# Hybrid attention decoder step on one core: sample sums one step earlier, projection's first block split anew, state copies inside the projection's loop

## The reference, cut to what matters

```python
def mixer_prompt(h, w_in, cw, g_sb, g_nsa, w_out):
    q_sb, k_sb, v_sb, q_n, kv_c, kv_s, kv_w, gates = project(h, w_in, pos)   # z = h @ w_in
    o_sb = sb_prompt(q_sb, k_sb, v_sb)                                        # stick-breaking attention
    ...                                                                       # compressed, selected and window attention
    out = mixer_out(o_sb, o_n, g_sb, g_nsa, w_out)

def sb_attend(q, k, v, q_pos, k_pos):
    z = jnp.einsum('bqhd,bshd->bhqs', q, k) / math.sqrt(HEAD_DIM)
    mask = k_pos[None, :] < q_pos[:, None]
    log_1m = jnp.where(mask, jax.nn.log_sigmoid(-z), 0.0)
    after = lax.cumsum(log_1m, axis=3, reverse=True) - log_1m
    a = jnp.where(mask, jnp.exp(jax.nn.log_sigmoid(z) + after), 0.0)
    return jnp.einsum('bhqs,bshd->bqhd', a, v)

# samples: the same over the gathered pages of the caches, and
win_all = jnp.concatenate([win_buf, kv_w], axis=1)
new_win_kv_sample = win_all[:, W + T - n_keep:]        # the window state, shifted by one row
```

## Time and profile before

| | us |
|---|---|
| median of 3 runs | 1145.65 |
| lowest, highest | 1145.42, 1149.24 |
| the profiled execution | 1144.81 |
| its span in the trace | 1143.0 |
| PE busy in the span | 1061.2 (93%) |
| DVE, ACT, POOL busy | 619.5, 391.3, 63.3 |
| mean granted clock of TensorE | 0.943 of full |

### The profile page before, as it was taken

The page is one execution under the profiler, slowest core; times in us unless marked ns, Lnnn a source line. Parts: engine busy times, 40 slices in busy tenths (PEclk is TensorE's granted clock), DMA queues, the critical chain, the costliest instruction groups (busy, mean ns, idle before and its releaser), DMA issues.

```text
span 1143.0 us, 22964 instructions
## 1 busy us (share of the span) xinstructions
PE 1061.2 (93%) x8284; PEld 933.5 (82%) x8284; DVE 619.5 (54%) x1056; ACT 391.3 (34%) x729; POOL 63.3 (6%) x83
## 2 busy tenths in 40 slices
PE   6899998988989998899999889999999999998995
PEld 5899997887878886555555558999999999998995
DVE  5334664777768776775455445445533335553334
ACT  4111122333333335656454354322221112222124
POOL 1000003111111100000000000100000000000000
PEclk8899996989989895999998999999999999999998
DMA  8427539999999853356666762223333332333221
GB/s 295 151 89 201 129 98 227 250 248 258 269 261 260 246 182 120 121 175 226 204 208 194 214 203 75 75 74 92 110 92 91 92 83 84 91 92 93 90 78 75
DMA packets 180323, 177.59 MB, mean 155 GB/s; under 512 B 13128, under 2 KB 140869, under 8 KB 177893
## 3 DMA queue, kind: packets, MB, share of 16 engines
q1 hardware_dynamic: 178536, 169.72, 52.5%
q10 hardware_dynamic: 1724, 7.04, 1.8%
HBM read 170.83 MB, written 10.06 MB: 158 GB/s over the span
## 4 chain that ended last, share of the span: by engine, by line
PE 61%; SPq 18%; issue 7%; DVE 5%; DMA 5%; ACT 3%; ACTq 1%; POOL 0%; DVEq 0%; POOLq 0%
PE bank L664 59%; SPq L578 4%; SPq L499 3%; SPq L542 3%; SPq L545 3%; PE bank L668 3%; SPq L492 2%; DMA high_arena<-in_w_in_dram 2%; SPq L566 2%; DMA low_arena<-in_cache_nsa_slc_kv_dram 1%; DMA low_arena<-in_consts_dram 1%; DMA high_arena<-out_cmp_p_dram 1%; ACTq L1284 1%; DVE high_arena L2231 0%; DMA high_arena<-in_cache_nsa_slc_kv_dram 0%
## 5 line engine op out<-in xcount | busy, mean ns | idle before, releaser
L664 PE MATMUL bank<-high_arena 128*128 128x254 f32 (+8 forms) x1864 | 242.0, 349 | 11.9 <-ACT high_arena L1321 6.1
L664 PEld LDWEIGHTS bank<-high_arena 128*128 128x128 f32 (+5 forms) x1864 | 186.9, 153 | 49.8 <-issue 9.2
L2163 DVE TENSOR_TENSOR w_low<-high_arena,w_high 128x1024 fp32r<-128x1024 f32 x72 | 90.1, 1252 | 81.0 <-ACT w_high L1484 71.0
L1484 ACT ACTIVATE w_high<-high_arena 128x1024 fp32r<-128x1024 f32 x72 | 76.4, 1061 | 144.7 <-PE bank L664 144.7
L668 PE MATMUL bank<-low_arena 128*128 128x128 f32 (+3 forms) x658 | 103.2, 298 | 16.4 <-DMA low_arena<-in_cache_nsa_slc_kv_dram 10.4
L664 PE MATMUL bank<-a_high,w_high 128*128 128x256 f32 (+1 forms) x512 | 103.7, 284 | 5.3 <-issue 2.9
L668 PEld LDWEIGHTS bank<-low_arena 128*128 128x128 f32 (+3 forms) x658 | 83.0, 157 | 28.9 <-issue 12.3
L664 PE MATMUL bank<-h_high,w_high 128*128 128x256 f32 (+1 forms) x512 | 103.0, 282 | 1.8 <-DVE h_low L2187 1.8
L664 PE MATMUL bank<-a_low,w_high 128*128 128x256 f32 (+1 forms) x512 | 103.2, 283 | 0.0
L664 PE MATMUL bank<-h_low,w_high 128*128 128x256 f32 (+1 forms) x512 | 103.2, 283 | 0.0
L664 PE MATMUL bank<-h_high,w_low 128*128 128x256 f32 (+1 forms) x512 | 103.1, 283 | 0.0
(11 more groups left out here) (227 smaller groups left out, 1541.2 us busy)
## 6 DMA issues: line engine op xcount, KB each, us to landing
low_arena<-in_cache_sb_kv_dram SPq DMA_DIRECT2D x128, 256.0 KB, 4.8
high_arena<-in_cache_sb_kv_dram SPq DMA_DIRECT2D x128, 256.0 KB, 3.5
high_arena<-in_cache_nsa_cmp_kv_dram SPq DMA_DIRECT2D x128, 128.0 KB, 5.0
high_arena<-in_w_up_dram SPq DMA_DIRECT2D x32, 512.0 KB, 4.0
high_arena<-in_w_down_dram SPq DMA_DIRECT2D x32, 512.0 KB, 4.0
high_arena<-in_w_in_dram SPq DMA_DIRECT2D x10, 1136.0 KB, 5.9
low_arena<-in_cache_nsa_slc_kv_dram SPq DMA_DIRECT2D x128, 64.0 KB
high_arena<-in_cache_nsa_slc_kv_dram SPq DMA_DIRECT2D x128, 64.0 KB, 2.3
```

The source lines that it names most:

```text
L664: return T.matmul(out, lhsT=l, rhs=r, start=start, stop=stop, **k)
L1484: S.activation(w_hi_r[u], w_raw[u], ACT.Copy).then_inc(sem(f"w_hi{u}"), 1)
L2163: V.tensor_tensor(w_lo_r[u], w_raw[u], w_hi[u], ALU.subtract).then_inc(sem(f"w_lo{u}"), 1)
```

## The change

Three independent parts.

1. **First block of the projection.** The low parts are cut into four pieces of two k each: DVE k 0 and 1, ahead of its `gained_low` loop (and no longer within it), POOL k 2 and 3, then k 4 and 5, then k 6 and 7. PE waits for `w_lo0` at k = 0 and for `z_zero` 2, 3, 4 at k = 2, 4, 6.
2. **State copies.** The eight copies leave their place ahead of the loop; one is issued by ACT behind the eviction of rows 3 of each of blocks 0 to 7.
3. **Steps.** `sample_sums`, `sample_logs` go from step 3 to step 2, the Exp and the memset of bank 7 from step 4 to step 3, the first pairs from step 5 to step 4. Samples 0 to 3 keep 3, 3, 2 pairs in three steps each, one step earlier; sample 4 has 3, 1, 1, 1, 0, 1, 0, 1 in steps 16 to 23 where it had 2 and six times 1 in steps 17 to 23. From step 24 on the table is as before.

```diff
-    at = 5
+    at = 4
...
-        for n in ((3, 3, 2) if b < 4 else (2, 1, 1, 1, 1, 1, 1)):
+        for n in ((3, 3, 2) if b < 4 else (3, 1, 1, 1, 0, 1, 0, 1) if b == 4 else (2, 1, 1, 1, 1, 1, 1)):
...
                         if k == 0:
-                            pe.wait_ge(sem("z_zero"), 2)
-                        if k == KD // 2:
                             pe.wait_ge(sem("w_lo0"), 1 + 1)
+                        elif k % 2 == 0:
+                            pe.wait_ge(sem("z_zero"), k // 2 + 1)
...
-                if s == 3:
+                if s == 2:
                     sample_sums()
...
-            for b in range(B):
-                act.dma_start(wo[b, 0:WIN - 1].rearrange("(o s) k h d -> o (s k h d)", o=1),
-                    wb[b, 1:WIN].rearrange("(o s) k h d -> o (s k h d)", o=1)).then_inc(sem("kv_out"), 16)
+            def window_rows(b):
+
+                act.dma_start(wo[ds(b, 1), 0:WIN - 1].rearrange("o s k h d -> o (s k h d)"),
+                    wb[ds(b, 1), 1:WIN].rearrange("o s k h d -> o (s k h d)")).then_inc(sem("kv_out"), 16)
+
...
                     win_high(1, i + turn)
                     z_out(0, i, turn, col)
+                    window_rows(i * 2 + 2 * turn)
                     win_high(0, i + turn + 1)
                     z_out(1, i, turn, col)
+                    window_rows(i * 2 + (2 * turn + 1))
...
-                if s == 4:
+                if s == 3:
                     act.wait_ge(*signal("s_d", 1))
...
+            dve.wait_ge(*signal("w_hi_first", 1))
+            V.tensor_tensor(win_r[0][:, 0:2], win[0][:, 0:2], win_hi[0][:, 0:2], ALU.subtract).then_inc(sem("w_lo0"), 1)
             for k in range(KD):
                 gained_low(k)
-                if k == 2:
-                    dve.wait_ge(sem("w_hi0"), 1)
-                    V.tensor_tensor(win_r[0][:, KD // 2:], win[0][:, KD // 2:], win_hi[0][:, KD // 2:], ALU.subtract).then_inc(sem("w_lo0"), 1)
...
                 if s == 3:
                     cmp_groups()
-                if s == 4:
                     dve.wait_ge(*signal("s_d", 1))
                     V.memset(bank[7][:, :], 0.0).then_inc(sem("samples_dve"), 1)
+                if s == 4:
                     rank_greater()
...
-                if s == 3:
+                if s == 2:
                     sample_logs()
...
-            G_.tensor_tensor(win_r[0][:, 0:KD // 2], win[0][:, 0:KD // 2], win_hi[0][:, 0:KD // 2], ALU.subtract).then_inc(sem("z_zero"), 1)
+            G_.tensor_tensor(win_r[0][:, 2:4], win[0][:, 2:4], win_hi[0][:, 2:4], ALU.subtract).then_inc(sem("z_zero"), 1)
+            pool.wait_ge(sem("w_hi0"), 1)
+            G_.tensor_tensor(win_r[0][:, 4:6], win[0][:, 4:6], win_hi[0][:, 4:6], ALU.subtract).then_inc(sem("z_zero"), 1)
+            G_.tensor_tensor(win_r[0][:, 6:8], win[0][:, 6:8], win_hi[0][:, 6:8], ALU.subtract).then_inc(sem("z_zero"), 1)
```

More of the change, by code:

```diff
@@ L163 @@
     "start_act": ["rt"] * 5 + ["w_hi_first", "gates_e"],
-    "samples_pe": ["c_sc", "g_mm", "m_T", "c_scT", "m_b", "c_pT", "s_c", "c_imp", "c_selT", "c_mask", "m_den", "m_T", "m_b", "m_den", "v_ss"],
-    "samples_dve": ["s_abs", "m_max", "c_s", "c_kbd", "m_diag", "s_sp", "c_nm", "m_sub", "s_suf", "c_p", "m_sum", "c_pg", "s_d", "acc_set", "c_sel",
+    "samples_pe": ["c_sc", "g_mm", "m_T", "c_scT", "m_b", "s_c", "c_pT", "c_imp", "c_selT", "c_mask", "m_den", "m_T", "m_b", "m_den", "v_ss"],
+    "samples_dve": ["s_abs", "m_max", "c_s", "c_kbd", "m_diag", "s_sp", "c_nm", "m_sub", "s_suf", "c_p", "m_sum", "s_d", "c_pg", "acc_set", "c_sel",
                     "c_selx", "c_selm", "m_max", "m_rec", "m_diag", "m_sub", "m_sum", "m_rec", "w_set", "v_sq", "v_st", "v_cols"],
```

## The result

The changed kernel took 1152.88 us in the median against 1146.55 for the kernel before on the same chip: ratio 1.0051, 95% interval [1.0026, 1.0075]. Measured again on another occasion it took 1148.0 against 1146.9: 1.0023 [0.9988, 1.0057]. The forecast's sum was +1.5 us, where the first measurement gives +5.8 (3.0 to 8.6) and the second +2.6 (-1.4 to +6.5). The time lies in the range of 1137 to 1156, a little above the 1142 to 1151 that the prediction gave to its own mechanism. The direction is right in the first measurement, the second doesn't tell it from no change; the forecast size is too small.

A forecast was written before the change was run, and what follows sets the result against it. The prediction took PE, with little slack to the loads, to bound most projection blocks, and SP's issuing the later steps. Its terms -1.6 - 4.6 + 8.5 - 0.8 = +1.5 gave 1147 us, range 1137 to 1156.

The forecast's parts named there:

- its own mechanism: Projection loads delayed by state copies, by 1.0 to 1.9 us each, steps near zero: 1142 to 1151 us, chance 0.50.
- The copies come back: Projection, blocks 1 to 8: each copy delays a load by 1.5 us; PE waits in seven further blocks, +8.5 us.
- Block 1 keeps 1.1 of its 5.7: Projection: wait of 3.02 and lower clock of 2.67 go, a wait of 1.1 us comes instead, -4.6 us.
- Part 1, -1.6: Start of the projection: PE starts near 16.1 and ends its first eight k near 22.3, not 23.96; -1.6 us.
- Part 3, -0.8: Steps: SP's issuing of quads begins 0.8 us earlier, so the last load and what follows come earlier; -0.8 us.
- Rival 1: Projection: copies pass beside the loads without delaying PE; sum -8.1 us, 1137.5 us, chance 0.22.
- Rival 2: Projection: eight loads beside copies land later than the copy's engine time says, 2.1 us or more; 1152 us, chance 0.16.
- Rival 3: Steps: a pause ahead of `sb_qk(4)` and a lower clock delay SP's issuing; +2 to +5 us, 1151 us, chance 0.12.
- Wrong as a whole if the projection's end moves by more than 4 us: Projection: the forecast fails as a whole if its end, 166 us before, moves over 4 us either way.

The follow-up runs named there:

- before, again: The kernel before, run once more unchanged for a second profile; ratio 1.0013.
- part 3 alone: Kernel before with only the steps' change (sample sums, logs, Exp, memset and first pairs one step earlier); ratio 1.0021.
- sums only: Kernel before with sample sums, logarithm, Exp and memset one step earlier, the table of pairs as before; ratio 1.0030.
- changed, again: The changed kernel, run once more unchanged for a second profile; 1148.0 us against 1146.9, ratio 1.0023.
- parts 1 and 2: The changed kernel with the steps of before, keeping the new first block and the copies in the loop; ratio 1.0027.
- the runs with no, half and moved copies: Changed kernel with the eight state copies left out (0.9961), cut to their first 256 rows (0.9993), or issued behind ACT's high part (0.9941).
- the moved copies: Changed kernel with each state copy issued behind ACT's high part of a block, whose load has just landed; 1139.84 us, ratio 0.9941.
- the two pairs that differ by part 3 alone: Changed kernel with new and old steps (1.0023, 1.0027); the same with each copy behind ACT's high part (0.9941, 0.9946).
- part 2 alone: Kernel before with only the state copies moved into the loop, one behind each block's eviction of rows 3; ratio 1.0117.

## Why the prediction was right, and why its size was too small

The projection's code of before ran in four profiles (before, again, part 3 alone, sums only) and that of the change in three (changed, again, parts 1 and 2):

| | end | PE busy | idle |
|---|---|---|---|
| before, mean of four | 164.46 | 150.56 | 13.90 |
| changed, mean of three | 169.42 | 149.39 | 20.03 |
| difference | +5.0 | -1.2 | +6.1 |

5.0 of 1146 us is 0.44%, which lies in the intervals of the changed kernel, of its second measurement and of parts 1 and 2. So the projection accounts for the whole of the loss that can be shown. Forecast for it was -1.6 - 4.6 + 8.5 = +2.3. By the prediction's steps:

- **The copies come back, +8.5: right, a little high.** The mechanism (a copy falls into a load) is shown by the runs with no, half and moved copies. The delay was taken as 1.5 and is 7.0 - 5.5 = 1.5, or 1.4 load by load. That it fits so closely is partly luck: 1.5 was the time of a packet when only copies ran, and beside a load a packet took 1.24. The seven waits are 0.78 to 1.32, together 7.43. In the three executions they are 7.7 in the mean, against 0.4 in the same places of the four before, so +7.3, and about +7.8 with the clock. The clock held behind them in the profiled execution, but not always: the second profile of the changed kernel has a wait of 2.11 at 104.00 behind a landing of 8.06, with matmuls of 1.70 after it. The rule of the Trainium skill that the prediction weighed (DMA: Bandwidth & Descriptors, section "Issuing engines are not separate DMA queues"), that transfers from different issuers run on the same engines and interleave, agrees with this trace: the two queues had 62.1% and 45.2% of the engines in the same two microseconds.
- **Block 1 keeps 1.1 of its 5.7, -4.6: the term that was mis-sized, twice.** First, 5.7 was 3.02 of waiting and 2.67 of lower clock in one execution. In the four executions the wait was 3.02, 1.86, 3.19 and 2.48, in the mean 2.64, because the load landed after 7.57, 6.22, 7.89 and 6.47, and the clock fell in two of them only (PE busy 151.81 and 152.05, against 149.21 and 149.17). What could be won was thus about 2.64 + 1.4 = 4.0, not 5.7. Second, what came in its place was not 1.1: this load landed in 8.38, 8.06 and 8.34 in the three executions, and PE waited 2.45, 2.12 and 2.40. Together 1.7 + 1.2 = 2.9 too much was put down as gained, and this is what made the forecast too small. With it, with 0.3 less gained by part 1 and 0.7 less lost to the copies, the sum for the projection is +4.8, for 5.0 measured.
- **Part 1, -1.6: right, -0.9 in the profiled pair and -1.3 in the means.** The samples' matmuls behind the first eight k come at 22.95 in the mean of the three changed executions and at 24.22 in that of the four before. DVE's piece took 0.75, as said. But DVE's products don't all follow at 0.68 each: the third waited 0.70 for ACT's `h_high`, because ACT makes the second half's high part in between. And of POOL's pieces, forecast at 1.3, the first took 1.96 and the other two 1.40 each.
- **Part 3, -0.8: no effect within some 0.3%.** Its details in the steps came out near the forecast: sums of 7.0 forecast, 6.06 measured; a pause of 2.5 ahead of `sb_qk(4)`, 2.43 measured; the pause of 2.31 gone, 0.36 left. From its first `sb_qk` PE reaches `sb_qk(4)` after 470.65 - 445.77 = 24.9 us, before after 460.80 - 436.77 = 24.0, so 0.9 later, not 2. SP's first quad is issued 564.13 - 445.77 = 118.4 after it, before 553.58 - 436.77 = 116.8, and in the two repeats 115.7 for the changed kernel and 117.8 for the one before: the 0.8 that should have been gained there are smaller than the difference from one execution to the next.
- **Rivals.** Rival 1, copies that pass beside loads, is refuted by eight waits; the moved copies give nearly its time, 1139.84 for the 1137.5 put down for it. Rival 2, a later landing at all eight loads, had 1152, and 1152.88 was measured; but only its number fits. Its later landing came true for the first load (8.1 to 8.4, a delay of 2.6 to 2.9) and sometimes for a later one (8.06 and 7.69 in the second profile). Rival 3, the steps, isn't seen in the two pairs that differ by part 3 alone; its upper 5 us would have shown there, its lower 2 would not.
- **"Wrong as a whole if the projection's end moves by more than 4 us":** it moved by 3.15 in the profiled pair and by 5.0 in the means. By the means this sign came true, because of the term of block 1. One profile of before, which can lie anywhere from 162.35 to 166.77, couldn't carry a limit of 4.
- **Luck.** The sum was +1.5, out of terms of -4.6 and +8.5 that were each off by 0.7 to 2.9. That its sign was right proves little; what bears the mechanism is that the eight waits stand where they were put, seven of them near the size they were given.

## What to carry to other kernels

A transfer without urgency belongs where the queue of loads is empty for longer than the transfer takes, here right behind the landing of a load; one issued half a microsecond behind a load delayed it by about its own time on the engines each time, and PE waited for all of that but the load's 0.4 us of slack. Before a wait and its lower clock are put down as a gain, the same place should be read in more than one execution, since the wait here varies from 1.9 to 3.2 and the fall of the clock comes in half of them. And a stretch of one profile (here 258.6 to 266.4 us for the same work) can't decide on an edit worth 1 or 2 us.

## What the runs showed of the hardware that I had not expected

- **A wait may cost nothing beyond itself, or 1.6, or 2.7 us more.** Behind a wait for the third block's load the distance to the next samples' matmuls, less the wait there, was 13.8 to 13.9 after waits of 1.86, 2.12, 2.40, 2.45 and 2.48, 15.4 to 15.5 after 2.35 and 3.38, and 16.5 to 16.7 after 3.02 and 3.19. The length of the wait alone doesn't tell: 2.45 left the clock at its higher level, while 1.91 at 122.60 in the run of part 2 alone was followed by the lower one.
- **The first load with a copy beside it lands later than the others:** 8.06 to 8.38 with a whole copy, where the other seven of the changed kernel's first profile took 6.66 to 7.28, but 6.15 with half a copy, like its neighbours. The copy's share of the engines doesn't explain it: its data are through by 41.4, and the load lands at 43.70 with the engines nearly empty. The DMA queues from 41 to 44 us in the changed kernel (packets, MB, share of 16 engines) show what else is there:

```profile
q1 hardware_dynamic: 118, 0.12, 12.2%
q8 instruction: 1, 0.02, 2.2%
```

One packet of an instruction queue took 2.2% of 48 us of engine time, 1.06 us on one engine, and from 42.4 on only eight packets of the load are left. Such a packet lies in the tail of this load in all four profiles whose copies stand as in the change, and in the profile shown here in none of the other seven loads. With half a copy it comes when the load is nearly through. So the load may wait for the one engine that is busy with instructions. No run was made for it, and the cause isn't shown.
- **Open: the stretch of pages.** PE's waits there for the loads of the nsa_slc cache were 20.7, 12.9, 15.2, 15.5, 11.9 and 14.3 us in the six kernels with the new steps, and 10.4, 11.1, 11.2, 6.5, 10.6, 9.3 and 8.2 in the seven without all of them; the stretches are 273.9 and 270.8 us long in the mean. The two groups don't overlap in the waits, although the instructions of this stretch are the same. Yet the times of the two pairs that differ by this part alone agree (1.0023 and 1.0027; 0.9941 and 0.9946), so it either is chance or is given back later. I have no mechanism and no run that tells.
